# Block inverse of an RWKV-7 chunk on 32x32 diagonal blocks instead of 64x64 ones

## What is computed

```
S = S * d_t - (S @ kk_t) b_t^T + v_t k_t^T        y_t = S @ r_t
```

## Time and profile before

| | |
|---|---|
| median of 3 runs | 1226.12 us (1221.83 to 1230.08) |
| profiled execution | 1221.72 us, its span 1219.9 us |
| mean granted TensorE clock | 0.982 |
| busy: PE, POOL, DVE, ACT | 94%, 49%, 39%, 25% of the span |
| inverse levels and the state work between them | about 276 to 434 us |

### The profile page before, as it was taken

How to read it: one execution, slowest core, us unless ns; L and a number is a source line. 1 busy time by engine, 2 the same in 40 slices (tenths; PEclk the granted TensorE clock), 3 DMA queues, 4 the chain that set the end, 5 groups by cost and what they waited for, 6 DMA issues and landing times.

```text
span 1219.9 us, 25961 instructions
## 1 busy us (share of the span) xinstructions
PE 1152.4 (94%) x10621; PEld 1086.3 (89%) x10629; DVE 481.0 (39%) x838; ACT 305.7 (25%) x585; POOL 593.0 (49%) x773
## 2 busy tenths in 40 slices
PE   4888989989999989999999999999999999999994
PEld 2876889888888889878889999999999999999994
DVE  5235185974254448986234433222100022220113
ACT  4223333443233343333350122222000012110101
POOL 3542265652122215643326655565565565565662
PEclk8999999999699999999999999999999999999998
DMA  5333442221000033122223222222222222222222
GB/s 198 92 75 63 71 96 84 63 72 38 19 21 3 4 101 104 53 69 78 71 91 109 78 77 72 70 77 77 70 78 77 69 78 77 70 77 78 71 69 87
DMA packets 47176, 89.23 MB, mean 73 GB/s; under 512 B 6600, under 2 KB 9040, under 8 KB 46896
## 3 DMA queue, kind: packets, MB, share of 16 engines
q1 hardware_dynamic: 42656, 76.70, 21.0%
q10 hardware_dynamic: 4432, 11.22, 4.2%
HBM read 80.06 MB, written 7.83 MB: 72 GB/s over the span
## 4 chain that ended last, share of the span: by engine, by line
PE 83%; DVE 10%; issue 3%; POOL 2%; ACT 1%; DMA 0%; DVEq 0%; SPq 0%; POOLq 0%; ACTq 0%
PE acc L624 37%; PE acc L625 24%; PE wk L740 3%; PE acc L806 2%; PE acc L804 2%; PE acc L792 1%; PE wk L624 1%; DVE invs L1844 1%; PE wk L625 1%; PE wk L650 1%; PE wk L1090 1%; PE acc L1063 1%; PE wk L1074 1%; PE wk L768 1%; PE acc L757 1%
## 5 line engine op out<-in xcount | busy, mean ns | idle before, releaser
L546 POOL TENSOR_TENSOR w_lo<-w_raw,w_hi 128x512 fp32r<-128x512 f32 x242 | 324.3, 1340 | 20.1
L543 POOL TENSOR_TENSOR w_hi<-w_raw,ones_w 128x32 fp32r<-128x32 f32 x242 | 67.8, 280 | 429.4 <-PE acc L625 409.5
L624 PE MATMUL acc<-h_hi,w_hi 128*128 128x384 f32 x584 | 207.0, 354 | 21.5 <-DVE kxs L1746 9.3
L624 PE MATMUL acc<-h_lo,w_hi 128*128 128x384 f32 x584 | 198.7, 340 | 0.0
L624 PE MATMUL acc<-h_hi,w_lo 128*128 128x384 f32 x584 | 198.7, 340 | 0.0
L625 PE MATMUL acc<-h_hi,w_hi 128*128 128x256 f32 x584 | 164.0, 281 | 0.0
L625 PE MATMUL acc<-h_lo,w_hi 128*128 128x256 f32 x584 | 164.0, 281 | 0.0
L625 PE MATMUL acc<-h_hi,w_lo 128*128 128x256 f32 x584 | 163.8, 281 | 0.0
L544 POOL TENSOR_SCALAR w_hi<-w_raw 128x480 fp32r<-128x480 f32 x242 | 149.1, 616 | 0.0
L624 PEld LDWEIGHTS acc<-h_hi,w_hi 128*128 128x128 f32 x584 | 110.6, 189 | 32.0 <-issue 14.0
L625 PEld LDWEIGHTS acc<-h_hi,w_hi 128*128 128x128 f32 x584 | 110.9, 190 | 0.4
(11 more groups left out here) (383 smaller groups left out, 2229.5 us busy)
## 6 DMA issues: line engine op xcount, KB each, us to landing
w_raw<-w SPq DMA_DIRECT2D x242, 256.0 KB, 2.6
line_scratch<-line ACTq DMA_DIRECT2D x8, 384.0 KB
xT<-xT SPq DMA_DIRECT2D x4, 640.0 KB, 6.0
x<-xT ACTq DMA_DIRECT2D x1, 2560.0 KB, 8.9
y<-x ACTq DMA_DIRECT2D x8, 320.0 KB, 2.6
bias_p<-line_scratch SPq DMA_DIRECT2D x8, 256.0 KB, 4.3
kc<-k_cache SPq DMA_DIRECT2D x8, 256.0 KB, 2.6
vc<-v_cache SPq DMA_DIRECT2D x8, 256.0 KB, 2.7
```

The source lines that it names most:

```text
L543: nc.gpsimd.tensor_tensor(w_hi[:, s, 0:LEAD], w_raw[:, r, 0:LEAD], ones_w[:], ALU.mult).then_inc(w_high, 1)
L546: nc.gpsimd.tensor_tensor(w_lo[:, s, :], w_raw[:, r, :], w_hi[:, s, :].bitcast(F32), ALU.subtract).then_inc(w_split, 1)
L624: mm(out[:, 0:CUT], w_, x_[:, k0 + b, 0:CUT], start=go, stop=end)
```

## The change

The inverses are kept as four 32x32 diagonal blocks (`invs` becomes [128, 2, 2, 4, 32], partition block b = 0..3 of 32 rows, "compact columns") for all levels up to blocks of 32. Products of these levels are 32x32x32, one for each block, so a part has 16 products for each p and an update 32. Copies by ACT and additions by DVE are half as wide. The full 64x64 transposed inverse is a new tile, `solve`: DVE writes the first inverse there, `pe_first` turns it (16 products with 32 columns) and also copies its diagonal blocks into compact form (4 products with 128 columns). The last level multiplies with the coupling block alone (8 products for a part, 8 for an update, each p); `pe_diagonal` (4 products with 128 columns for each p) puts the diagonal blocks back at their places in PSUM; DVE then writes `solve` with one masked copy. Tile 0 has no last level, but gets the diagonal and the masked copy as one more step of `update_mm` and `inv_set`.

```diff
-    invs = [at(f"invs{q}", W0 + (22.25, 4)[q], [P, 2, 2, 4, HD]) for q in range(2)]
-    part = at("part", W0 + 8, [P, NH, HD])
+    invs = [at(f"invs{q}", W0 + (22.25, 4)[q], [P, 2, 2, 4, HB]) for q in range(2)]
+    solve = [at(f"solve{q}", W0 + (24.25, 6)[q], [P, 2, 4, HD]) for q in range(2)]
+    part = at("part", W0 + 8, [P, NH, HB])
...
+            def block(b):
+                return slice(HB * b, HB * b + HB)
...
@@ pe_first
-                        for c in range(2):
-                            done = mm(acc[half(c), p, 512 + j * HD:512 + (j + 1) * HD], invs[i % 2][half(c), p, 1, j, :],
-                                      ident[half(c), half(c)], start=True, stop=True)
+                        for b in range(4):
+                            mm(acc[block(b), p, 512 + j * HB:512 + (j + 1) * HB], solve[i % 2][block(b), p, j, block(b % 2)],
+                               ident[block(b), block(b)], start=True, stop=True)
+                    for b in range(4):
+                        done = mm(acc[block(b), p, 640:768].rearrange("q (j d) -> q j d", j=4), ident[block(b), block(b)],
+                                  solve[i % 2][block(b), p, :, block(b % 2)], start=True, stop=True)
...
@@ pe_part
-                    for c in range(2):
-                        done = mm(acc[half(c), p, j * HD:(j + 1) * HD], merge[n % 2][half(c), 4 * p + j, :],
-                                  invs[i % 2][half(c), p, 0, j, :], start=True, stop=True)
+                    for b in (range(4) if level < 4 else (0, 2)):
+                        to, cols = (b, b % 2) if level < 4 else (b + 1, 1)
+                        done = mm(acc[block(to), p, j * HB:(j + 1) * HB], merge[n % 2][block(b), 4 * p + j, block(cols)],
+                                  invs[i % 2][block(b), p, 0, j, :], start=True, stop=True)
...
@@ pe_update
+                if level == 4:
+                    for j in range(4):
+                        for b in (1, 3):
+                            at_ = 512 + j * HD + HB
+                            done = mm(acc[block(b - 1), p, at_:at_ + HB], part[block(b), 4 * p + j, :], inv_t[block(b), j, :],
+                                      start=True, stop=True)
+                else:
+                    for j in range(4):
+                        for b in range(4):
+                            if i or level < 2:
+                                mm(acc[block(b), p, 512 + j * HB:512 + (j + 1) * HB], inv_t[block(b), j, :],
+                                   part[block(b), 4 * p + j, :], start=True, stop=True)
+                            done = mm(acc[block(b), p, 640 + j * HB:640 + (j + 1) * HB], part[block(b), 4 * p + j, :],
+                                      inv_t[block(b), j, :], start=True, stop=True)
...
+            def pe_diagonal(i, p):
+                pe.wait_ge(inv_set, 2 * added(i, 3 if i else 2) + p + 1)
+                for b in range(4):
+                    out = acc[block(b), p, 512:768].rearrange("q (j d) -> q j d", j=4)[:, :, block(b % 2)]
+                    done = mm(out, ident[block(b), block(b)], invs[i % 2][block(b), p, 1, :, :], start=True, stop=True)
+                if not i:
+                    done.then_inc(update_mm, 1)
...
@@ dve_inverse
+                if level == (4 if i else 3):
+                    mask = e_masks[:, E_LT + P * (i == 0) + HD:E_LT + P * (i == 0) + P]
+                    do(V.tensor_tensor(solve[i % 2][:, p], acc[:, p, 512:768].rearrange("q (j d) -> q j d", j=4), over_heads(mask, 4),
+                                       ALU.mult), inv_set)
+                    return
```

More of the change, by code:

```diff
@@ L32 @@
 HD = 64
+HB = 32
 NH = 8
@@ L192, in stage, with added, inverted @@
     return (5 * i - 2 if i else 0) + level
+def added(i, level):
+    return stage(i, level) + (1 if i else 0)
+def inverted(i):
+    return 2 * added(i, 5 if i else 4)
 def g_sets(i):
@@ L784, in pe_part @@
                 if level:
-                    pe.wait_ge(inv_set, 2 * (n - 1) + p + 1)
+                    pe.wait_ge(inv_set, 2 * added(i, level - 1) + p + 1)
                 else:
@@ L794, in pe_part @@
                 done.then_inc(part_mm, 1)
             def pe_update(i, level, p):
-                n, last = stage(i, level), level == merges(i) - 1
-                pe.wait_ge(part_set, 2 * n + p + 1)
+                pe.wait_ge(part_set, 2 * stage(i, level) + p + 1)
                 inv, inv_t = invs[i % 2][:, p, 0], invs[i % 2][:, p, 1]
[L801 to L807, removed]
@@ L934, in _ @@
                     pe_update(0, level, p)
+            for p in range(2):
+                pe_diagonal(0, p)
             pe_from_v(0)
@@ L961, in _ @@
                 for p in range(2):
+                    if level == 4:
+                        pe_diagonal(1, p)
                     pe_part(1, level, p)
@@ L1012, in _ @@
                     for p in range(2):
+                        if level == 4:
+                            pe_diagonal(following, p)
                         pe_part(following, level, p)
@@ L1019, in _ @@
             pe_from_v(i)
-            pe.wait_ge(inv_set, 2 * stage(i, merges(i)))
+            pe.wait_ge(inv_set, inverted(i))
             pe_from_state(i, 0, 0)
@@ L1393, in act_first @@
                     act.wait_ge(first_turned, 2 * i + p + 1)
-                    do(A(columns(invs[i % 2][:, p, 0]), acc[:, p, 512:768], ACT.Copy), inv_first)
+                    do(A(invs[i % 2][:, p].rearrange("q n j d -> q (n j d)"), acc[:, p, 512:768], ACT.Copy), inv_first)
             def act_part(i, level):
@@ L1398, in act_part @@
                     act.wait_ge(part_mm, 2 * stage(i, level) + p + 1)
-                    do(A(columns(part[:, 4 * p:4 * p + 4, :]), acc[:, p, 0:256], ACT.Copy), part_set)
+                    do(A(columns(part[:, 4 * p:4 * p + 4, :]), acc[:, p, 0:4 * HB], ACT.Copy), part_set)
             def act_g(i, rows):
@@ L1837, in dve_inverse @@
             def dve_inverse(i, level, p):
-                dve.wait_ge(update_mm, 2 * stage(i, level) + p + 1)
-                if level == merges(i) - 1:
-                    dst, src = invs[i % 2][:, p, 1].rearrange("q j d -> q (j d)"), acc[:, p, 768:1024]
+                dve.wait_ge(update_mm, 2 * added(i, level) + p + 1)
+                if level == (4 if i else 3):
[3 more added lines that the diff above has]
+                    return
+                if level == 2 and not i:
+                    dst, src = invs[i % 2][:, p, 1].rearrange("q j d -> q (j d)"), acc[:, p, 640:768]
                 else:
-                    dst, src = invs[i % 2][:, p].rearrange("q n j d -> q (n j d)"), acc[:, p, 512:1024]
+                    dst, src = invs[i % 2][:, p].rearrange("q n j d -> q (n j d)"), acc[:, p, 512:768]
                 do(V.tensor_tensor(dst, dst, src, ALU.add), inv_set)
@@ L1900, in _ @@
                 dve_pairs(0, 1, p)
-            for level in range(merges(0)):
+            for level in range(merges(0) + 1):
                 for p in range(2):
```

8 lines of the change are left out of this document (4 added, 4 removed).

## The result

The changed kernel is slower: a median of 1258.91 us over 4 runs (1257.60 to 1264.13), against 1223.97 us for 4 runs of the kernel before (1219.17 to 1230.08). The ratio is 1.0291 [1.0233, 1.0348]. The prediction of 1210 us (1196 to 1245) was wrong in sign, and the time lies above its range.

What follows compares the result with a forecast made beforehand. TensorE, busy 94% of the span, was taken as the bound; tiles 2 to 4 -11 us, tile 1 -2.5, tile 0 -2, sum -15.5: 1206 from the profiled 1221.7, stated as 1210 for the median, range 1196 to 1245.

Steps and rivals of the forecast that it cites:

- the price of a pass: 32-column passes on four TensorE pieces in the RWKV stage: 8 ns each taken, between 7 and 29 ns.
- Rival A: Supply of passes to TensorE limits, 14 to 16 ns a pass; +2.5 us, about 1229; chance 0.20.
- the point at which the change turns to a loss: Price of a pass above which the whole change was forecast to lose time: about 14 ns.
- rival B: TensorE's clock falls through the inverse with 32-row, 32-column passes, 14.5 ns each; +22 us, 1247; chance 0.15.
- Levels 2 and 3: Inverse of tiles 2, 3 and 4: 2.15 us a level, 4.3 for two instead of 6.52, -2.2 us.
- Level 4: Last level of the inverse, tiles 2 to 4: 2.1 us instead of 2.61, -0.5 us a tile.
- Changes of piece: TensorE switching between 32-row and 64-row pieces, eight more times per tile: about 0.12 us each, +1.0 us.
- Rival C: Four pieces on TensorE overlap no better than two, 29 ns a pass; +53 us, 1278; chance 0.10.
- DVE, ACT and POOL: In the RWKV stage: DVE's masked copy and POOL cost nothing; DVE's addition 0.42 us, ACT's copy 0.28 us.
- The loads of the earlier trace: TensorE weight loads of 16, 64 and 128 columns, 90, 145 and 192 ns, read as 0.8 to 0.9 ns a column.

Runs made afterwards that it cites:

- probe_end: Kernel before plus unused TensorE passes behind its last product, four hardware loops and one written-out list; only its trace counts, not its 1391.36 us.
- skip_plain: Changed kernel without the update of the plain inverse in levels 2 and 3 of tiles 1 to 4; 1249.93 us, ratio to before 1.0202.
- looped_levels: Changed kernel with levels 2 and 3 of tiles 2 to 4 as one hardware loop body run twice; 1242.79 us, ratio to before 1.0210.
- before_bf16: Kernel before with 64x64 blocks and BF16 operands of turning, parts and updates; 1208.92 us, ratio to before 0.9913.
- last_only_again: Kernel before with only the new off-diagonal last level, on 64x64 inverses, rerun in five rounds; 1216.83 against 1219.11 us, ratio 0.9987.

## Why the prediction was wrong

**The failed step** is the price of a pass, "I take 8 ns", where it stands for a whole level. As the price of passes that are there it was right: 8.9 ns in probe_end's loop and in the burst at 403.71, and 10.4 ns in an update (the 64 passes from 407.82 on). As a sustained price it is wrong: the straight list of probe_end gets 128 passes in 3.5 to 4.0 us, 27 to 31 ns each. Rival A had this mechanism and priced it at 14 to 16 ns, half of what it is, by the assumption that passes would "come no faster per column than now". Its "for" already named the right row, with a level that "would want 384 instructions, 25 kB, four times that rate". Its "against", "the queue's share is 1.4%", was a misreading: that is the share of 16 DMA engines' time, and says nothing about how closely packets that come singly can follow one another. The row to read was the number of packets by the length of the stretch: 6 or 7 in 31 us is one in 4.4 to 5.2, not far from what turned out to be the limit. A count of the changed tile would have given its time: 1,274 passes are 2,548 instructions, 10 packets, 37 us at 3.70 us each, and 38.6 were measured. The prediction put the point at which the change turns to a loss at 14 ns, and the sustained price is twice that.

For the stage as a whole the packets alone are not the time: 48 x 3.70 = 178 of 208 us, and 32 x 3.70 = 118 of 173 before. Before, the supply had room; after, most of it is used up, and each packet taken away again gives some 3 us (skip_plain 11.7 / 4, looped_levels 12.5 / 4, each give or take 1 us).

**The clock** fell (0.76 in the stage instead of 0.94), as rival B said, and the forecast, which priced tiles 2 to 4 at full clock, had that wrong too (0.81 in this tile). B held the shape of the passes for the cause, and the shape alone does not do it. In probe_end's loop passes of 32 rows and columns ran, with no more than the 0.31 us between turns, for 42.1 us at 1.00; in its written-out list the same passes fell to half at 1366.2, just behind the first hole of 2.42 us. And before_bf16, where the levels have 64-row pieces only, stands at 0.81, with TensorE waiting 12.9 us for DVE's additions. In these rows the fall comes with idle time between bursts. In the kernel before it did not: there the clock fell at 312.4, behind the samples' passes, with one hole of 0.31 us in the 17 us ahead. So what makes it fall is not settled. What it cost can only be estimated: 531 passes on `64*64` pieces ran at half clock, against 217 before, (531 - 217) x 25 ns = 8 us by the burst at 431.07. 2,001 passes on `32*32` pieces ran at half clock too, an update's at 14.5 ns (415.28) instead of 10.4 (407.82), which is at most 8 us more, as far as the supply did not hide it. So of the 34.7 us, 24.0 are idle time, nearly all of it "issue"; the 10.8 us of longer busy time can be the clock, passes that trickle in with holes shorter than their modelled tail of 0.2 us, or both, and how much of the forecast gain is set off against them stays open. The second turn in looped_levels shows that supply alone makes the holes; no run held the clock and left the supply as it was.

**Levels 2 and 3**: 2.15 us each was forecast, and 2.1 for level 4. In tile 3, from the first pass of each part to that of the next, they take 3.20, 7.07 and 2.53 us; level 3 has the two holes of about 2 us. Together that is 12.80 instead of 9.13 us:

```profile
418.20:421.40 3.20, 2.34 (x194) 2.04 (x192) 0.43 (x2) 1.51 (x4) 1.27 (x1) 1.00 0.00 0
421.40:428.47 7.07, 3.14 (x200) 2.84 (x193) 1.61 (x4) 0.65 (x3) 0.00 (x0) 0.61 0.02 5
428.47:431.00 2.53, 2.35 (x100) 2.07 (x89) 1.25 (x5) 0.55 (x2) 1.04 (x1) 0.50 0.02 6
```

**Level 4**: it took 2.53 us, at half clock, against 2.61 before, where 2.1 was forecast. Its narrow part and update alone are worth nothing that can be measured (last_only_again); the forecast's -0.5 us a tile would be about 0.1% of the kernel, too little to be seen.

**Changes of piece** came out as forecast: from the last pass on 64 rows (about 403.56) to the first on 32 (403.71) 0.15 us; back, 404.27 to 404.56, 0.29 where 0.2 was taken (0.15 and 0.21 in probe_end's fourth loop). So a change of piece costs little here.

**Rival C**, 29 ns a pass, gives 1278 and comes nearest in its price, with the wrong cause: it held the array for the limit. The page behind it, "TensorE: Matmul & The Clock Gate" (Part 1) of the Trainium skill, says that start-to-start never drops below about 25 ns however small N is. The trace disagrees for the array as a whole (8.9 ns over four pieces, so 36 ns between two starts on the same piece) and comes close to that number where a straight list limits it, and in probe_end's loop on 64x64 pieces, where 29.2 ns is the mean of steps of 7 and 52 ns.

**DVE, ACT and POOL** cost nothing, as forecast: the times of one instruction of DVE and ACT fit (0.42 and 0.28 us), and in the stage both wait for TensorE, as POOL does with its merges.

**Two readings in the prediction** are off without changing its outcome. The loads of the earlier trace rows are (145 - 90) / 48 = 1.1 ns a column from 16 to 64 columns and (192 - 145) / 64 = 0.7 ns from 64 to 128, not 0.8 to 0.9 throughout. And the sums of rivals C and B, 53 and 22 us on top of 1226, give 1279 and 1248, one more than the prediction has.

In one sentence: the mechanism of the forecast (narrow weights, four pieces, shorter additions) was there, and a limit that the kernel before had not shown as a wait, the pace at which instructions come, took it away and cost 35 us on top, part of them perhaps through the clock.

## What to carry to other kernels

Before work is cut into smaller pieces to make each cheaper, count the instructions. Where a straight list asks TensorE for more than about 256 instructions in 3.7 us, that is a pass with its weight load in less than some 29 ns, the time goes in these runs by the count and not by the size of the pieces; packets on the instruction queue per stretch, and waits on "issue" without a releaser, are the rows that show it. If small pieces are wanted all the same, either a product must need fewer passes, or the list must be a loop whose body is fetched once. In looped_levels the second turn of a level took 2.90 us at half clock, where the level before took 3.14 to 3.38 us at full clock.

## What the runs showed that was not expected

- The body of a hardware loop runs without packets: 3,072 passes of probe_end's third loop with none on the queue. There is a gap of 0.31 us between its turns; the loops of 64x64 pieces show none.
- Halving the moving columns alone does not make an fp32 pass cheaper: 29.2 and 29.1 ns for 64 and 32 moving columns on 64x64 pieces. With 32-column weights on four pieces side by side it is 8.9 ns. (128 moving columns do cost more: 28 passes on `32*64` pieces in 1.58 us, 56 ns each.)
- The granted clock stayed at 1.00 through 42.1 us of dense passes on 32x32 pieces, and fell to half in the same passes with holes between them.
